# A gated feed-forward product recast as seven quarter products per unit, with tokens stationary and gated tiles turned on TensorE

## The reference, cut to what matters

```
def swiglu(hn, w_ffn_in, w_ffn_out):
    a, b = jnp.split(hn @ w_ffn_in, 2, axis=-1)
    return (jax.nn.silu(a) * b) @ w_ffn_out
...
        ff = swiglu(rmsnorm(h, norm_ffn_pre[l]), w_ffn_in[l], w_ffn_out[l])
        h = h + rmsnorm(ff, norm_ffn_post[l])
```

## Time and profile before

| | us |
|---|---|
| median of 3 runs | 1602.05 |
| lowest, highest | 1601.84, 1603.89 |
| the profiled execution, its own time | 1600.48 |
| its span, first to last instruction | 1598.7 |
| PE busy in it | 1302.3 (81%) |
| DVE busy | 395.3 (25%) |
| ACT busy | 166.2 (10%) |
| mean granted clock of TensorE | 0.945 |

### The profile page before, as it was taken

How to read it: one execution, slowest core, us unless ns; L and a number is a source line. 1 busy time by engine, 2 the same in 40 slices (tenths; PEclk the granted TensorE clock), 3 DMA queues, 4 the chain that set the end, 5 groups by cost and what they waited for, 6 DMA issues and landing times.

```text
span 1598.7 us, 25596 instructions
## 1 busy us (share of the span) xinstructions
PE 1302.3 (81%) x11430; PEld 884.0 (55%) x11430; DVE 395.3 (25%) x852; ACT 166.2 (10%) x331; POOL 41.2 (3%) x84
## 2 busy tenths in 40 slices
PE   5999877556655656665565999999999999999998
PEld 4786454334333333333333776788544686788853
DVE  2236422111111111111112022223544201211243
ACT  4114200000000000000001032200111100100000
POOL 1201000000000000000001000000000000000000
PEclk9999999898888898888988999999999999999999
DMA  9958789999999999999999433334333443444441
GB/s 367 383 190 305 324 364 429 432 431 431 429 431 432 430 429 430 432 432 430 429 431 412 173 106 106 106 106 158 123 140 122 142 137 126 158 158 158 158 158 53
DMA packets 86585, 447.33 MB, mean 280 GB/s; under 512 B 3916, under 2 KB 35824, under 8 KB 72064
## 3 DMA queue, kind: packets, MB, share of 16 engines
q1 hardware_dynamic: 84256, 441.20, 68.9%
q10 hardware_dynamic: 1008, 3.74, 0.6%
q0 software_dynamic: 1264, 1.55, 0.5%
HBM read 445.41 MB, written 1.06 MB: 279 GB/s over the span
## 4 chain that ended last, share of the span: by engine, by line
issue 86%; PE 9%; DMA 2%; DVE 1%; POOL 1%; POOLq 0%; DVEq 0%; SPq 0%; ACT 0%
PE PS L1550 3%; PE PS L1536 2%; DMA mem<-in_w_mod 2%; PE PS L1621 2%; PE PS L1483 1%; PE PS L1475 0%; PE PS L1723 0%; DVE mem L943 0%; DVEq L934 0%; PE PS L1682 0%; DVE mem L974 0%; POOL mem L547 0%; DVE mem L933 0%; POOL mem L494 0%; PE PS L1610 0%
## 5 line engine op out<-in xcount | busy, mean ns | idle before, releaser
L1723 PE MATMUL PS<-mem 128*32 128x192 f32 x4096 | 183.4, 333 | 107.8 <-DMA mem<-in_w_up 53.6
L1731 PE MATMUL PS<-mem 128*32 128x256 f32 x1536 | 144.7, 553 | 125.6 <-DMA mem<-in_w_down 119.8
L1723 PEld LDWEIGHTS PS<-mem 128*32 128x32 f32 x4096 | 138.5, 112 | 156.1 <-issue 69.1
L1731 PEld LDWEIGHTS PS<-mem 128*32 128x32 f32 x1536 | 64.3, 154 | 198.2 <-DMA mem<-in_w_down 130.3
L1766 PE MATMUL PS<-mem 128*128 128x256 f32 (+1 forms) x768 | 172.7, 385 | 0.8 <-DVE mem L1170 0.8
L1766 PEld LDWEIGHTS PS<-mem 128*128 128x128 f32 x768 | 144.9, 190 | 24.9 <-DVE mem L1170 1.2
L2069 PE MATMUL PS<-mem 128*128 128x256 f32 x640 | 138.3, 379 | 0.0
L2069 PEld LDWEIGHTS PS<-mem 128*128 128x128 f32 x640 | 121.5, 190 | 16.5
L1949 PE MATMUL PS<-mem 128*128 128x512 f32 x224 | 98.4, 594 | 0.7 <-ACT mem L788 0.7
L1111 DVE TENSOR_TENSOR mem<-mem,PS 128x192 f32<-128x192 f32 x32 | 11.3, 354 | 256.1 <-ACT mem L695 256.1
L1949 PEld LDWEIGHTS PS<-mem 128*128 128x128 f32 x224 | 41.9, 190 | 53.3 <-issue 51.8
(11 more groups left out here) (320 smaller groups left out, 1235.8 us busy)
## 6 DMA issues: line engine op xcount, KB each, us to landing
mem<-in_w_gate SPq DMA_DIRECT2D x32, 3072.0 KB, 38.0
mem<-in_w_up SPq DMA_DIRECT2D x32, 3072.0 KB, 40.9
mem<-in_w_down SPq DMA_DIRECT2D x32, 3072.0 KB, 38.6
mem<-in_w_in SPq DMA_DIRECT2D x26, 2048.0 KB, 8.3
mem<-in_w_mod SPq DMA_DIRECT2D x12, 2048.0 KB, 16.6
mem<-in_w_ffn_in SPq DMA_DIRECT2D x22, 1024.0 KB, 6.6
mem<-in_w_ffn_out SPq DMA_DIRECT2D x5, 2048.0 KB, 7.8
mem<-in_w_ret_out SPq DMA_DIRECT2D x4, 2048.0 KB, 8.2
```

The costliest lines, as they stand in the source:

```text
L1723: last = mm(PS[32 * gg:32 * gg + 32, 2 * h + 1, 192 * j:192 * j + 192], xTe[:, h, c, :], w[:, o:o + 192], start=c == 0 and j == 0, stop=c ...
L1731: last = mm(PS[32 * gg:32 * gg + 32, 2 * h, 0:256], hTe[:, h, j, :], slots[:, 3 * h + 2, o:o + 256], start=j == 0, stop=j == JE - 1, skip_ ...
```

## The change

Units 1 to 10 of the first product are recast. For a unit, the tokens are split into two tiles of 128, K into two halves of 512, and the outputs into gate and up of 256 columns each. The 2x2 by 2x2 block product is made with seven products m1 to m7, each of four calls with 128 tokens stationary and 256 weight columns moving. Four token combinations `fi_x` are made once, on DVE, and three weight combinations `fi_w` and one in place for each unit (`in_weights`, in three steps). The products that belong to one running sum share a bank ("p": m1, m6, m5, m3), and ACT copies out the stages m1, u2 = m1 + m6 and u4 = u2 + m5 between them; DVE adds the copies to the other banks ("q": m2, "r": m7 and m4). That gives a0 and a1 (gate rows of token tile 0 and 1) and b1; b0 is read from bank "p" itself. ACT applies silu, DVE multiplies to g0 and g1, and since these have tokens on partitions, PE turns their four 128x128 tiles (`g_T`) in the next unit, and ACT copies them to `gT`. Unit 0 stays. The release of an "fi" chunk is now m4 of its unit. `out_weights(0)` stands behind c22 of unit 10, `out_weights(1)` behind g1 of unit 10, and the second product's banks are renumbered. The tables `fi_pe`, `fi_act`, `fi_dve` and `combos` give the count of each event on its semaphore.

```
 FIRST_STEP, N_UNITS = 11, 38
+FI = FB // 2
 FO_CHUNKS, FO_MAIN = 6, 4
 FO_FROM = 1 + 4 * RH
...
         mixpost = late.take(D)
...
+        fi_w = [[shaped(mem[:, o + D * k:o + D * k + D], 4, 256) for k in range(3)] for o in (at_hn, at_rows)]
+        fi_x = [shaped(part[:, CW * k:CW * k + CW], 4, P) for part in (flat(vmbuf), flat(sTm)) for k in range(2)]
+        fi_temps = [flat(ysbT)[:, 256 * i:256 * i + 256] for i in range(8)]
+        m1_half, u2_half, u4_half, b1_half = fi_temps[0:4]
+        a0_half, a1_half = fi_temps[4:6], fi_temps[6]
...
+        def counted(start, events):
+            return {event: start + n + 1 for n, event in enumerate(events)}
+        def fi_order(head, each, last):
+            return head + [e for j in range(1, FI) for e in each(j)] + last
+        fi_pe = counted(8 * RH, fi_order(
+            [("m1", 1), ("m2", 1)],
+            lambda j: [("m6", j), ("m7", j), ("m5", j)] + [("turned", j - 1)] * (j > 1)
+            + [("m1", j + 1), ("m2", j + 1)] * (j + 1 < FI) + [("m3", j), ("m4", j)],
+            [("turned", FI - 1)]))
+        fi_act = counted(4 * RH, fi_order(
+            [("m1", 1)],
+            lambda j: [("a1", j - 1)] * (j > 1) + [("a0", j), ("u2", j), ("u4", j)] + [("g", j - 1)] * (j > 1)
+            + [("m1", j + 1)] * (j + 1 < FI),
+            [("a1", FI - 1), ("g", FI - 1)]))
+        fi_dve = counted(3 * RH, fi_order(
+            [("c11", 1)],
+            lambda j: [("c21", j - 1), ("g1", j - 1)] * (j > 1) + [("c22", j)] + [("c11", j + 1)] * (j + 1 < FI) + [("g0", j)],
+            [("c21", FI - 1), ("g1", FI - 1)]))
+        combos = counted(FO_FROM, fi_order(
+            [("fi_x", 0), ("fi_w", 1), ("x", 0)],
+            lambda j: [("fi_w", j + 1) if j + 1 < FI else ("w", 0)] + [("x", j - 1)] * (j > 1),
+            [("w", 1), ("x", FI - 1)] + [("w", i) for i in range(2, FO_CHUNKS)] + [("row0", 0), ("c22", 0), ("c21", 0)]))
...
+        def fi_bank(what, j):
+            return {"p": (0, 4), "q": (1, 5), "r": (2, 6), "t": (7, 3)}[what][j % 2]
...
         for i in range(FB // 2):
-            stream("fi", i, w_fi[:, :, :, i * 256:(i + 1) * 256], (KD, 2, 256), "ff_psum", i + 1)
+            stream("fi", i, w_fi[:, :, :, i * 256:(i + 1) * 256], (KD, 2, 256), "prod_psum" if i else "ff_psum",
+                   fi_pe["m4", i] if i else 1)
...
-            for j in range(FB // 2):
-                a.wait_ge(S["ff_psum"], j + 1)
-                if j >= 2:
-                    a.wait_ge(S["ff_ready"], j - 1)
-                a.activation(ff_tmp[:, j % 2, :], PS[:, 2 * (j % 2), :], ACT.Silu).then_inc(S["ff_silu"], 1)
+            a.wait_ge(S["ff_psum"], 1)
+            a.activation(ff_tmp[:, 0, :], PS[:, 0, :], ACT.Silu).then_inc(S["ff_silu"], 1)
+            def half_copy(dst, what, j, bank):
+                a.wait_ge(S["prod_psum"], fi_pe[what, j])
+                a.activation(dst, PS[:, bank, 0:256], ACT.Copy).then_inc(S["prod_copied"], 1)
+            def half_silu(buf, what, j):
+                a.wait_ge(S["prod_added"], fi_dve[what, j])
+                a.activation(buf, buf, ACT.Silu).then_inc(S["prod_copied"], 1)
+            def turned_g(j):
+                a.wait_ge(S["prod_psum"], fi_pe["turned", j])
+                a.activation(flat(gT[:, 2 * j:2 * j + 2, :]), PS[:, fi_bank("t", j), :], ACT.Copy).then_inc(S["prod_copied"], 1)
+            half_copy(m1_half, "m1", 1, fi_bank("p", 1))
+            for j in range(1, FI):
+                if j > 1:
+                    half_silu(a1_half, "c21", j - 1)
+                half_silu(a0_half[j % 2], "c11", j)
+                half_copy(u2_half, "m6", j, fi_bank("p", j))
+                half_copy(u4_half, "m5", j, fi_bank("p", j))
+                if j > 1:
+                    turned_g(j - 1)
+                if j + 1 < FI:
+                    half_copy(m1_half, "m1", j + 1, fi_bank("p", j + 1))
+            half_silu(a1_half, "c21", FI - 1)
+            turned_g(FI - 1)
...
-            for j in range(FB // 2):
-                if j == FB // 2 - 1:
+            g0_half, g1_half = fi_temps[7], ff_tmp[:, 1, 0:256]
+            (x11, x21), (x12, x22) = [[hnT[:, k:k + 4, P * t:P * t + P] for t in range(TT)] for k in (0, 4)]
+            s1, s2, s3, s4 = fi_x
+            v.drain()
+            v.tensor_tensor(s1, x21, x22, ALU.add)
+            v.tensor_tensor(s3, x11, x21, ALU.subtract)
+            v.drain()
+            v.tensor_tensor(s2, s1, x11, ALU.subtract)
+            v.drain()
+            v.tensor_tensor(s4, x12, s2, ALU.subtract).then_inc(S["combined"], 1)
+            def in_weights(j, step):
+                w, (t3, t2, t4) = chunk2("fi", j), fi_w[j % 2]
+                if step == 0:
+                    chunk2_landed(v, "fi", j)
+                    v.tensor_tensor(t3, w[:, 4:8, 1, :], w[:, 0:4, 1, :], ALU.subtract)
+                    v.drain()
+                elif step == 1:
+                    v.tensor_tensor(t2, t3, w[:, 0:4, 0, :], ALU.add)
+                    v.tensor_tensor(w[:, 0:4, 1, :], w[:, 0:4, 1, :], w[:, 0:4, 0, :], ALU.subtract)
+                    v.drain()
+                else:
+                    v.tensor_tensor(t4, w[:, 4:8, 0, :], t2, ALU.subtract).then_inc(S["combined"], 1)
+            def half_added(dst, copy, copied, product, bank, j):
+                v.wait_ge(S["prod_copied"], fi_act[copied, j])
+                v.wait_ge(S["prod_psum"], fi_pe[product, j])
+                v.tensor_tensor(dst, copy, PS[:, bank, 0:256], ALU.add).then_inc(S["prod_added"], 1)
+            for step in range(3):
+                in_weights(1, step)
+            v.wait_ge(S["ff_silu"], 1)
+            v.tensor_tensor(flat(gT[:, 0:2, :]), ff_tmp[:, 0, :], PS[:, 1, :], ALU.mult).then_inc(S["ff_ready"], 1)
+            out_sums(0)
+            half_added(a0_half[1], m1_half, "m1", "m2", fi_bank("q", 1), 1)
+            for j in range(1, FI):
+                if j > 1:
+                    half_added(a1_half, u2_half, "u2", "m4", fi_bank("r", j - 1), j - 1)
+                if j + 1 < FI:
+                    in_weights(j + 1, 0)
+                if j > 1:
+                    v.wait_ge(S["prod_copied"], fi_act["a1", j - 1])
+                    v.tensor_tensor(g1_half, a1_half, b1_half, ALU.mult).then_inc(S["prod_added"], 1)
+                if j + 1 < FI:
+                    in_weights(j + 1, 1)
+                v.drain()
+                half_added(b1_half, u4_half, "u4", "m7", fi_bank("r", j), j)
+                if j + 1 < FI:
+                    in_weights(j + 1, 2)
+                else:
                     out_weights(0)
-                v.wait_ge(S["ff_silu"], j + 1)
-                v.tensor_tensor(flat(gT[:, 2 * j:2 * j + 2, :]), ff_tmp[:, j % 2, :], PS[:, 2 * (j % 2) + 1, :], ALU.mult)\
-                    .then_inc(S["ff_ready"], 1)
-                out_sums(j)
-            for i in range(1, FO_CHUNKS):
+                if j > 1:
+                    v.wait_ge(S["prod_copied"], fi_act["g", j - 1])
+                    out_sums(j - 1)
+                if j + 1 < FI:
+                    half_added(a0_half[(j + 1) % 2], m1_half, "m1", "m2", fi_bank("q", j + 1), j + 1)
+                v.wait_ge(S["prod_copied"], fi_act["a0", j])
+                v.wait_ge(S["prod_psum"], fi_pe["m3", j])
+                v.tensor_tensor(g0_half, a0_half[j % 2], PS[:, fi_bank("p", j), 0:256], ALU.mult).then_inc(S["prod_added"], 1)
+            half_added(a1_half, u2_half, "u2", "m4", fi_bank("r", FI - 1), FI - 1)
+            v.wait_ge(S["prod_copied"], fi_act["a1", FI - 1])
+            v.tensor_tensor(g1_half, a1_half, b1_half, ALU.mult).then_inc(S["prod_added"], 1)
+            out_weights(1)
+            v.wait_ge(S["prod_copied"], fi_act["g", FI - 1])
+            out_sums(FI - 1)
+            for i in range(2, FO_CHUNKS):
                 out_weights(i)
...
             v.drain()
-            product_added(4, fo_u2, 7, fo_u4)
-            v.drain()
-            product_added(5, fo_u4, 2, fo_rows[0][:, CW:D]).then_inc(S["combined"], 1)
+            product_added(4, fo_u2, 3, fo_u4)
+            v.drain()
+            product_added(5, fo_u4, 1, fo_rows[0][:, CW:D]).then_inc(S["combined"], 1)
...
-            for j in range(1, FB // 2):
+            g0_half, g1_half = fi_temps[7], ff_tmp[:, 1, 0:256]
+            s1, s2, s3, s4 = fi_x
+            def in_product(name, j):
+                w, (t3, t2, t4) = chunk2("fi", j), fi_w[j % 2]
+                bank, x, part, start, stop = {
+                    "m1": ("p", hnT[:, 0:4, 0:P], w[:, 0:4, 0, :], True, False), "m2": ("q", hnT[:, 4:8, 0:P], w[:, 4:8, 0, :], True, True),
+                    "m6": ("p", s2, t2, False, False), "m7": ("r", s3, t3, True, False), "m5": ("p", s1, w[:, 0:4, 1, :], False, False),
+                    "m3": ("p", s4, w[:, 4:8, 1, :], False, True), "m4": ("r", hnT[:, 4:8, P:2 * P], t4, False, True)}[name]
+                for c in range(4):
```

(67 more changed lines are left out.)

## The result

The changed kernel takes 1591.53 us (median of 6 runs, 1590.36 to 1593.32) against 1601.94 us for the kernel before in the same set (6 runs, 1600.96 to 1604.8). The ratio is 0.9933, with a 95% interval of 0.9923 to 0.9944. The profiled execution's span went from 1598.7 to 1588.4 us.

What follows compares the result with a forecast made beforehand. TensorE was taken to bound the first product. Its stage falls from 138.13 to 127.1 us, 11.0 less, minus 0.44 for the last turning: 10.6 off 1602.05 gives 1591.4, range 1589 to 1597.5.

Steps and rivals of the forecast that it cites:

- PE's own work: First product: 560 passes at 0.216 us plus 4.4 us of turning, 125.4 us in place of 138.13.
- The waits in a unit: Units of the first product: hand-offs among PE, ACT and DVE lie beside PE's passes; u2's copy has 1.1 us cover.
- DVE: DVE's queue in each unit of the first product: busy 8.3 of 12.5 us, all beside PE's passes.
- The sentence in the rival: No-gain rival (chance 0.05), m6 waiting for weights: DVE must lose 5.1 us in a unit before the first tenth shows.
- Entry: Start of the recast units: token sums and unit 1's weights done at 1387.4, m6 due 1390.2; cost 0, cover 2.8 us.
- Weight loads: Weight chunks of the first product, slot released at m4: copies land in time, cost 0, cover 4.7 us.
- The hand-over: From unit 10 to the second product: PE waits for its first weight combination on DVE, 1.9 us, bounds 1.7 and 2.2.
- A hand-off exposed per unit: Rival, chance 0.08: ACT late to u2, m5 waits 0.64 us in each of ten units; 6.4 us, 1597.8.
- A turning pass at its shown length: Rival, chance 0.03: each turning pass costs 0.27 us, not 0.11; 6.4 us over 40 passes, 1597.8.
- The clock: Rival, chance 0.03: seven short groups on changing banks lower the first product's clock; two slow units of ten give 1616.5.

Runs made afterwards that it cites:

- the second set: The changed kernel run again, unaltered, as base for the follow-up runs on the same chip: 1590.64 us (5 runs) against 1602.8 us for the kernel before.
- the two doses: Changed kernel with two or four extra 512-column ACT copies per unit ahead of u2's copy: 1589.31 us and 1601.53 us.
- seven operations of 5.3 us: Changed kernel with seven extra 512-column DVE operations ahead of the last weight combination in units 1 to 9: 1600.28 us (8 runs).
- The split version: Changed kernel with the second product's first weight combination spread over unit 10 in three steps: 1588.39 us, ratio to the kernel before 0.9911.
- the doubled block: Changed kernel with each block of four turned tiles issued twice into the same bank: 1593.44 us.
- the run with ten operations: Changed kernel with ten extra 512-column DVE operations ahead of the last weight combination in units 1 to 9: 1628.62 us.
- The run that brought the clock back: The kernel with ten extra DVE operations, with m2 also made twice in each unit: 1619.88 us (2 runs) against 1628.62.

## Why the prediction was right

The span was put near 1588.1 us and came at 1588.4; the time at 1591.4, and it is 1591.53. The stage, put near 127.1 us and measured at 126.89 in two sets, shows that the working was right. That the median came within 0.2 us is in part luck, since in the second set the same kernel had 1590.64. The prediction's own range of 1589.5 to 1593.5 is also narrower than its terms: added up they give 1588.7 to 1594.6, unless one counts on their not falling together. Nothing hung on it.

**PE's own work.** Predicted: 560 passes at 0.216 and turnings at 0.44. The stage bears out both, and the roles of tokens and weights cost nothing: an eighth product per unit brings 17.27 us, exactly its passes. The difference is what the change took away, 17.3 us for a product per unit, less 4.4 for turning and 2.1 for two waits, which is 10.8; the stage and the last turning give 138.13 - 126.89 = 11.24, less 0.44, = 10.8.

**The waits in a unit.** Predicted as hidden, with u2 the tightest at 1.1 us. Right that it's hidden; the cover was counted from a copy as early as it can start. What ACT can still take in is larger, 1.6 us, since it also stands idle 0.5 us between the silus and m6's end, and the two doses fit the larger number: 1.3 us cost nothing, which is already more than 1.1, and 2.6 us cost 1.2, near the 1.0 above the cover and the 0.1 of the pass behind a wait.

**DVE.** Predicted as 8.3 of 12.5 us, with no cost: right. The operation that writes onto the chunk it reads (L1499) takes 1.22 us as the others do. The sentence in the rival, that DVE would have to lose 5.1 us in a unit before anything shows, was wrong. It took the slack of one result for that of the queue. The queue repeats each unit, so a delay comes round to c21 and c11 of the next; seven operations of 5.3 us, which should have cost 0.2 us per unit, cost 0.8.

**Entry.** m6 of unit 1 was put behind unit 1's weights with 2.8 us of cover. The weights were there at 1386.40 + 1.23 = 1387.63, 3.0 us before m6 was due at 1390.60, and the 96 passes from 1387.14 run without a break, so nothing showed.

**Weight loads.** Predicted as hidden with 4.7 us to spare. In all nine units DVE starts the next unit's first weight combination 0.34 us behind c21, without waiting for the chunk.

**The hand-over.** Predicted 1.9 us of stall and 0.2 for u4; measured 1.77 of stall, 0.19 for u4 and 0.10 in the pass behind that wait. The sum is still the predicted 2.1, because the end of DVE's work sets PE's start; the 0.10 was not in the working. The split version shows that the stall was the place of four DVE operations in the queue and nothing else: all 1.77 us came back.

**Rivals.** A hand-off exposed per unit: not there; 1.3 us of extra ACT work per unit do not make it, 2.6 us do. A turning pass at its shown length: excluded by the doubled block. The Trainium skill's 275 ns (TensorE: Matmul & The Clock Gate, Part 4: PE-mode transpose) is the duration, not what a block adds here. The clock: 1.00 in the stage. The rival took seven short groups on changing banks as its mechanism, and these, with their waits satisfied, never brought it down. In the run with ten operations it came down with idle times of 2.4 to 2.9 us in each unit.

## What to carry to other kernels

When a repeated unit is recast, lay it out on one clock: PE's order by pass spacing, each hand-off from rows (here 0.2, 0.02 and 0.06 us), each in-order queue summed over the whole unit. The cover of a queue is what is left of the unit after all its work, and not the slack of the one result that is due. Then look at the last unit, where the regular pattern ends: here the only new stall came from work put in one piece behind the last result, while the slots that the other units use for it stood empty.

## What was not expected of the hardware

TensorE's granted clock held at 1.00 over idle times of about 1 us in every unit (0.96 us after ACT, 0.68 to 1.49 us after DVE) and over the single wait of 1.6 us at the hand-over. With 2.4 to 2.9 us in every unit, it stood at 0.75 to 0.78 in the products behind them, in eight of nine units; in the ninth it held. (All of these are idle times as the view shows them.) The run that brought the clock back made PE's idle time shorter and gave it more work at once, so which of the two did it is not shown. One effect of it is that 17.3 us of needless passes made that kernel 8.75 us faster in the stage. The Trainium skill (TensorE: Matmul & The Clock Gate, HAM oscillation — how this bites in real kernels) describes such a swing for idle times between bursts of matmuls, with waits of 3 to 5 us for DMA in its example; these rows agree in kind, and here waits of 2.4 to 2.9 us were enough.
